# Two row tiles through each column group: a new opening for the projection stage of a hybrid decoder step

## The reference

```python
xn = rmsnorm(x, g_attn)                       # 1088 rows of 1024
z = xn @ w_in                                 # 1024 x 1952
cq  = rmsnorm(z[..., :256], g_q_a);   q = cq @ w_q_b          # 256 x 768, its last 32 columns a head rotated
ckv = rmsnorm(z[..., 256:384], g_kv_a); k, v = ckv @ w_uk, ckv @ w_uv   # 128 x 512 each
kr = rope(z[..., 384:416])                    # one key part for all heads
dq, dk, dv = rope(z[..., 416:928]), rope(z[..., 928:1440]), z[..., 1440:]
```

## Time and profile before

| | |
|---|---|
| Time, median of 3 runs (lowest to highest) | 1854.7 us (1853.81 to 1857.46) |
| The profiled execution | 1853.93 us, of which the span is 1852.4 |
| PE busy | 1733.5 us, 94% of the span |
| DVE, ACT, POOL busy | 861.0, 660.3, 573.8 us |
| First matmul of attention starts at | 281.07 us |

### The profile page before, as it was taken

How to read it: one execution, slowest core, us unless ns; L and a number is a source line. 1 busy time by engine, 2 the same in 40 slices (tenths; PEclk the granted TensorE clock), 3 DMA queues, 4 the chain that set the end, 5 groups by cost and what they waited for, 6 DMA issues and landing times.

```text
span 1852.4 us, 28046 instructions
## 1 busy us (share of the span) xinstructions
PE 1733.5 (94%) x9955; PEld 1509.9 (82%) x9955; DVE 861.0 (46%) x1802; ACT 660.3 (36%) x1329; POOL 573.8 (31%) x533
## 2 busy tenths in 40 slices
PE   3999988899996999999699999999999999999997
PEld 2788877888885888888578988898898888888985
DVE  5443325676773777667444233323333333233235
ACT  5222215576664766666322311112121121121213
POOL 0000003565662578678200312122122122131221
PEclk9999997999996999999899999999999999999998
DMA  7223213332315765654531495695875865956822
GB/s 254 83 95 103 84 55 105 94 95 55 100 34 143 197 195 157 164 149 132 178 110 29 114 171 106 132 145 130 149 118 131 172 103 113 167 122 135 135 55 101
DMA packets 156123, 227.41 MB, mean 123 GB/s; under 512 B 31127, under 2 KB 129048, under 8 KB 149592
## 3 DMA queue, kind: packets, MB, share of 16 engines
q1 hardware_dynamic: 153150, 159.39, 29.3%
q0 software_dynamic: 2880, 66.85, 22.1%
HBM read 201.12 MB, written 91.93 MB: 158 GB/s over the span
## 4 chain that ended last, share of the span: by engine, by line
PE 48%; DMA 2%; DVE 1%; ACT 1%; POOL 0%; issue 0%; ACTq 0%; SPq 0%; DVEq 0%; POOLq 0%
PE wide L2259 21%; PE turn L2281 14%; PE rest L2260 7%; PE wide L1942 5%; DMA acc<-in_w_gate 1%; DMA out_y_prompt<-f_gc 1%; PE wide L2357 0%; PE turn L1954 0%; DVE f_gc L2237 0%; ACT f_gc L2174 0%; DMA o_work<-scratch_s_o 0%; PE rest L2266 0%; DVE o_tl L1890 0%; POOL f_gl L2336 0%; ACT f_rows L2181 0%
## 5 line engine op out<-in xcount | busy, mean ns | idle before, releaser
L2194 DVE TENSOR_TENSOR acc<-turn,acc 128x512 f32<-128x512 f32 x198 | 136.6, 691 | 206.7 <-PE turn L2281 206.7
L2281 PE MATMUL turn<-f_dh,f_ah 128*128 128x512 f32 x396 | 158.3, 400 | 4.4 <-DVE f_al L2225 4.0
L2062 POOL TENSOR_TENSOR f_gl<-f_graw,f_gh 128x1024 fp32r<-128x1024 f32 x21 | 50.6, 2407 | 358.6 <-ACT f_gh L2112 358.6
L2281 PE MATMUL turn<-f_dl,f_ah 128*128 128x512 f32 x396 | 157.9, 399 | 0.0
L2281 PE MATMUL turn<-f_dh,f_al 128*128 128x512 f32 x396 | 157.9, 399 | 0.0
L2208 DVE SCALAR_TENSOR_TENSOR f_gc<-wide,f_coef,f_gc 128x832 f32<-128x832 f32 x44 | 47.7, 1085 | 209.3 <-ACT f_lasts L2132 206.4
L523 PE MATMUL zp<-win_h,xT_h 128*128 128x512 f32 (+1 forms) x288 | 112.6, 391 | 0.0
L1573 POOL TENSOR_TENSOR w_vl<-w_v,w_vh 96x2048 fp32r<-96x2048 f32 (+3 forms) x32 | 111.5, 3495 | 2.0
L523 PE MATMUL zp<-win_l,xT_h 128*128 128x512 f32 (+1 forms) x288 | 111.5, 387 | 0.0
L523 PE MATMUL zp<-win_h,xT_l 128*128 128x512 f32 (+1 forms) x288 | 111.4, 387 | 0.0
L2076 POOL TENSOR_TENSOR f_dl<-f_draw,f_dh 128x2048 fp32r<-128x2048 f32 x11 | 50.7, 4612 | 152.8 <-ACT f_dh L2152 152.8
(11 more groups left out here) (354 smaller groups left out, 4775.6 us busy)
## 6 DMA issues: line engine op xcount, KB each, us to landing
out_s_win_k<-in_state_win_k POOLq DMA_DIRECT2D x10, 3264.0 KB, 43.0
out_s_win_v<-in_state_win_v POOLq DMA_DIRECT2D x10, 3264.0 KB, 45.3
w_k<-in_state_win_k SPq DMA_DIRECT2D x16, 768.0 KB, 8.3
w_v<-in_state_win_v SPq DMA_DIRECT2D x16, 768.0 KB, 6.1
f_uraw<-in_w_up SPq DMA_DIRECT2D x22, 512.0 KB, 4.3
f_draw<-in_w_down SPq DMA_DIRECT2D x11, 1024.0 KB, 33.7
f_graw<-in_w_gate SPq DMA_DIRECT2D x21, 512.0 KB, 7.3
m_c<-in_cache_kv_latent SPq DMA_DIRECT2D x128, 64.0 KB, 1.8
```

Source lines behind the costliest of these rows:

```text
L2062: nc.gpsimd.tensor_tensor(w_lo[n][:], w_raw[n][:], w_hi[n][:].bitcast(F32), ALU.subtract)\
L2194: nc.vector.tensor_tensor(a, dp[h][:], a, ALU.add).then_inc(S["d_add"], 1)
L2281: last = nc.tensor.matmul(dp[h][:], a[:, c, t * P:(t + 1) * P], w[:, c, h * 512:(h + 1) * 512], start=(c == 0 and j == 0), stop=(c == 1 an ...
```

## The change

Only `project` changes. Five things:

- Tiles 0 and 1 go through each column group one after the other. Each has two banks: tile 0 uses `zp[0]` and `zp[1]` (groups 0 and 2, and 1 and 3), tile 1 uses `zp[2]` and `zp[3]`. From tile 2 on each group has its own bank as before.
- In tile 0 PE waits slice by slice, not group by group.
- On ACT and DVE the splits of the slices are woven between the other work of tiles 0 and 1. `w_uk` and `w_uv` now come before groups 2 and 3.
- The slots are four buffers of their own: `stage`, `dvm` (values), `turn` (rotation), `dqk`. `qm` and `km` are no slots any more. So queries and latents are built while slices still come; what is built in `dvm`, `turn` and `dqk` comes after slice 19. The sum of squares of tile 1 uses `dqk` as scratch, so slice 3 waits for it.
- SP issues what is needed first: `x` of tile 0, `g_x`, `ident`, `x` of tile 1, slices. The latents' gains and the rotary tables come later.

The loop `walk` then runs tiles 2 to 5, and 6 to 8 are written out.

```diff
+        banks = lambda t: [zp[i] for i in ((0, 1, 0, 1) if t.first else (2, 3, 2, 3) if t.second else range(4))]
-        need = {0: 4, 1: 8, "q": 10, 2: 14, 3: 18, "kv": 20}
+        need = {0: 0, 1: 4, "q": 10, "kv": 12, 2: 12, 3: 16}
+            return (stage, dvm, turn, dqk)[n % SLOTS][:, 0:a * b].rearrange("p (a b) -> p a b", a=a)
...
+                elif n == SLOTS - 1:
+                    sp.wait_ge(S["x_ms"], 2)
...
             def lead():   # scalar
-                square(Step.of(0))
-                weights(0, 4)
-                prep(Step.of(0))
-                weights(4, 8)
-                square(Step.of(1))
-                prep(Step.of(1))
-                weights(8, len(loads))
+                square(t0); square(t1); weights(0, 1); prep(t0); weights(1, 4); prep(t1); weights(4, 6)
+                sums(t0); weights(6, 8); latent_hi(t0); weights(8, 10); sums(t1); weights(10, 12)
+                key_turned(t0); query(t0); weights(12, 16); square(Step.of(2)); weights(16, 20)
+                act.wait_ge(S["w_lo"], len(loads))
+                key_value(t0); latent_hi(t1); key_turned(t1); query(t1); sliding_value(t0)
+                prep(Step.of(2)); square(Step.of(3)); key_value(t1); sliding_value(t1)
...
             def lead():   # vector, new
+                normalize(t0); weights(0, 1); normalize(t1); prep(t0); weights(1, 4); prep(t1); weights(4, 7)
+                latent(t0); weights(7, 8); latent_lo(t0); key_turned(t0); weights(8, 12)
+                latent(t1); query(t0); key_turned(t1); weights(12, 16); normalize(Step.of(2)); weights(16, 20)
+                dve.wait_ge(S["w_lo"], len(loads))
+                latent_lo(t1); sliding(t0, 0); sliding(t0, 1); query(t1); sliding(t1, 0)
+                prep(Step.of(2)); sliding(t1, 1); normalize(Step.of(3))
...
             def lead():   # tensor, new
+                prep(t0); prep(t1); rows_ready(t0); group(t0, 0); rows_ready(t1); group(t1, 0)
+                latent(t0); group(t0, 1); query(t0); group(t1, 1); key_value(t0); group(t0, 2)
+                latent(t1); group(t1, 2); query(t1); group(t0, 3); prep(Step.of(2)); key_value(t1); group(t1, 3)
```

More of the change, by code:

```diff
@@ L165, in project @@
 def project(nc, sem, io):
+    SLOTS = 4
     ctx = ExitStack()
@@ L214, in project @@
                               win_l[:, k0:k0 + 2, c0:c0 + n], (2, n)))
[L215 to L218, removed]
+        group_loads(0)
+        group_loads(1)
+        for k in range(2):
+            loads.append((io["w_q_b"].rearrange("(k p) n -> p k n", p=P)[:, k:k + 1], wqb_h[:, k:k + 1],
+                          wqb_l[:, k:k + 1], (1, HEADS * QK)))
         for i, n in enumerate(("w_uk", "w_uv")):
@@ L368, in prep, with sums @@
                     nc.scalar.copy(xT_h[t.odd][:, 4 * i:4 * i + 4, :], xp[i][:]).then_inc(S["xT_hi"], 1)
-            def main(t):
+            def sums(t):
+                z = banks(t)[0]
                 act.wait_ge(S["z0_ps"], t.n + 1)
@@ L487, in main, with sliding @@
-                if not ends(t):
-                    normalize(t.after_next())
+            def sliding(t, i):
+                dve.wait_ge(S[f"z{i + 1}_ps"], t.n + 1)
+                if not t.first:
+                    dve.wait_ge(S[("o_dq", "o_dk")[i]], t.n * 16)
+                if i == 1:
+                    dve.wait_ge(S["dq_ok"], t.n + 1)
+                elif not t.first:
+                    dve.wait_ge(S["dk_ok"], t.n)
+                rotate(heads(banks(t)[i + 1][:]), heads(dqk[:, i * HW:(i + 1) * HW]), heads(rt[0]), heads(rt[1]),
+                       rot[t.odd][:, 0:3 * RD], RD, "d_a", t.n * 6 + (3 * i + 3), ("dq_ok", "dk_ok")[i])
@@ L526, in product, with rows_ready, latent @@
                     last.then_inc(S[done], 1)
+            FREE = ("kr_ok", "dq_ok", "dk_ok", "dv_ok")
             def group(t, g):
                 c0, n = GROUPS[g]
-                if t.first:
-                    pe.wait_ge(S["w_lo"], need[g])
-                else:
-                    for s in (("kr_ok",), ("dq_ok",), ("dk_ok",), ("dv_ok",))[g]:
-                        pe.wait_ge(S[s], t.n)
-                product(zp[g][:, 0:n], [(xT_h[t.odd][:, k, :], xT_l[t.odd][:, k, :], win_h[:, k, c0:c0 + n],
-                                         win_l[:, k, c0:c0 + n]) for k in range(KC)], f"z{g}_ps")
-            def main(t):
+                z = banks(t)[g]
+                if t.first or t.second:
+                    if g >= 2:
+                        pe.wait_ge(S[FREE[g - 2]], t.n + 1)
+                else:
+                    pe.wait_ge(S[FREE[g]], t.n)
+                for k in range(KC):
+                    if t.first and k % 2 == 0:
+                        pe.wait_ge(S["w_lo"], need[g] + k // 2 + 1)
+                    xh, xl, wh, wl = (xT_h[t.odd][:, k, :], xT_l[t.odd][:, k, :], win_h[:, k, c0:c0 + n],
+                                      win_l[:, k, c0:c0 + n])
+                    for i, (a, b) in enumerate(((xh, wh), (xh, wl), (xl, wh))):
+                        last = nc.tensor.matmul(z[:, 0:n], a, b, start=(k == 0 and i == 0),
+                                                stop=(k == KC - 1 and i == 2))
+                last.then_inc(S[f"z{g}_ps"], 1)
+            def rows_ready(t):
                 pe.wait_ge(S["xT_lo"], t.n * 2 + 2)
-                group(t, 0)
-                group(t, 1)
+            def latent(t):
                 pe.wait_ge(S["cn_ok"], t.n + 1)
@@ L548, in main, with query @@
                 last.then_inc(S["cT_ps"], 1)
-                group(t, 2)
+            def query(t):
                 pe.wait_ge(S["cT_lo"], t.n + 1)
@@ L562, in main, with lead @@
                                                   wkv_l[:, c0:c0 + 512])], done)
-            staged(pe, prep, main)
+            def main(t):
+                rows_ready(t)
+                group(t, 0)
+                group(t, 1)
+                latent(t)
+                group(t, 2)
+                query(t)
+                group(t, 3)
+                key_value(t)
+            def lead():
+                t0, t1 = Step.of(0), Step.of(1)
+                prep(t0)
+                prep(t1)
+                rows_ready(t0)
+                group(t0, 0)
+                rows_ready(t1)
+                group(t1, 0)
+                latent(t0)
+                group(t0, 1)
+                query(t0)
+                group(t1, 1)
+                key_value(t0)
+                group(t0, 2)
+                latent(t1)
+                group(t1, 2)
+                query(t1)
+                group(t0, 3)
+                prep(Step.of(2))
+                key_value(t1)
+                group(t1, 3)
+                pe.wait_ge(S["dk_ok"], 1)
+                pe.wait_ge(S["dv_ok"], 1)
+            walk(pe, prep, main, lead)
 class Ring:
```

292 lines of the change are left out of this document (208 added, 84 removed).

## The result

The changed kernel takes 1835.12 us (median of 4 runs, 1830.51 to 1837.34) against 1854.26 us; the ratio is 0.9896, 95% interval 0.9875 to 0.9918. On another chip it came to 1834.12 against 1851.54, ratio 0.9915 (0.9888 to 0.9943). The forecast was 1836.1.

A forecast was written before the change was run, and what follows sets the result against it. PE was taken to set the projection phase's end; first product 16.6, work 52.6, stall 3.0, small waits 0.3 and clock 0.8 gave 73.3 against 91.9, so 1836.1 us, range 1829 to 1843.

The forecast's parts named there:

- What bounds the kernel: PE sets the end of the projection phase; whatever time tile 2 starts earlier, everything behind it starts earlier.
- T: Start of PE's transposes of tile 3, at 91.90 us before the change and forecast at 73.3.
- S: Start of tile 0's first product on PE, forecast at 16.6 us, with 15.6 and 17.6 as bounds.
- the bound of 10.2: Time in us for the cast of slice 0 if its load moves up by four small loads' issue; 11.0 was taken.
- The pause: PE's stall before tile 1's latents, waiting for ACT's copy of values behind the last splits; 3.0 us.
- The clock: Time lost to PE's lowered clock after the stall before tile 1's latents: 0 or 1.6 us, taken as 0.8.
- The sign set for being wrong: Granted clock of 0.50 for more than 7 us between the first product and tile 3's transposes.
- The sum: Start of tile 3's transposes: 16.6 + 52.6 + 3.0 + 0.3 + 0.8 = 73.3 us, a gain of 18.6.
- Slices too slow: Rival: DVE's eight late slices take 1.68 us each, stall 6.1, gain 13.7, about 1841 us; chance 0.18.
- no pause: Rival in the opening: first product at 15.6, stall 1, no clock loss, gain 22.4, 1832.3 us; chance 0.07.
- The clock stays low: Rival: PE's broken stream in the lead runs at 1.2 GHz, 26 us slower, 1881 us; chance 0.03.
- The entry of attention: Rival: the 17.0 us low clock there changes; at best 1829 us, at worst 1.3 us more; chance 0.08.

The follow-up runs named there:

- the value buffer: Against the changed kernel, tile 0's values get a buffer of their own and ACT copies them before slices 16 to 19; 1825.96 us, second run 1826.25.
- the second profile: The changed kernel itself, nothing altered, run and profiled again on another chip; 1834.12 us, ratio 0.9915 to the kernel before.
- the kernel with one tile at a time: Against the changed kernel, the pairing is undone: PE takes tile 0 through all its groups, then tile 1; 1839.85 us, ratio 0.9950 to before.
- the warm kernel: Against the early-start kernel, PE does ten unused transposes of the identity before the first product; 1824.33 us, second run 1824.58.
- the early-start kernel: Against the value-buffer kernel, tile 0's group 0 starts before tile 1 is normalized, with tile 1's transposes inside it; 1824.39 us, second run 1824.21.

## Why the prediction was right

*What bounds the kernel.* Right. PE's 52.64 us of work for two tiles behind the start gives T where there is neither a pause nor a low clock behind the start: 15.1 + 52.6 is 67.7 against 67.21 measured with the value buffer. And a shift of T is a shift of the end, as far as the medians tell.

*S.* Forecast 16.6, measured 15.25, below the lower bound of 15.6. The chain from the cast of slice 0 was sized right (5.48 for 5.6). The load was not: the cast came at 9.77 for 11.0. I had gone by bytes in the queue; with the old order of loads it came at 12.21, so the small and repeated loads (tables, gains) cost 2.4 us though they are 336 KB. SP issues slice 0's load at 2.89 for 4.79, so 1.9 of the 2.4 is the time to issue four loads, which I had worked out and used only as the bound of 10.2. The rows of tile 1 count too: they arrive at 8.72 for 10.95, and ACT squares them for 1.06 us just ahead of the cast.

*The pause.* Place, releaser and kind right; forecast 3.0, measured 4.15 and 3.68. The earlier S moves both ends of the pause, so they are counted from S: PE came after 30.95 us for the 31.5 forecast, and ACT's copy ended after 34.96 for 34.4. The four last splits took 1.28 us each, the pace I had taken and not the 1.68; but DVE waited 1.20 us ahead of them, and 0.84 in the second profile, for slices that were not there yet. The load of slice 16 was issued at 37.39, as soon as its slot was free, and took 5.5 us. The forecast had put this at nothing ("if slices are there when wanted"). Less this wait, an estimate, the pauses would have been 2.95 and 2.84 us.

*The clock.* Taken at 0.8 with 1.6 as the bound. Half of 4.51 us, 2.25, is what the first profile shows, and 1.65 the second (mean 0.64 over 4.60). Both are over the bound. It was half of the 3.20 us in which PE worked at 0.50 before; but there the clock had been low for some 3.6 us of the idle time already (mean 0.79 over 8.60), so less of the low time fell on work. The sign set for being wrong was more than 7 us at 0.50; with some 2 us inside the pause the low stretch of the first profile was about 6.8 us long.

*The sum.* 73.3 forecast, 73.99 and 72.81 measured. The misses cancel in part: S -1.35 and -1.5, the pause +1.15 and +0.7, the clock +1.45 and +0.85, PE's work and small waits -0.5 each time. That the sum is off by no more than 0.7 is in part luck. The gain on T was 18.6 forecast and is 17.9 and 19.1. Attention's first matmul came at 263.72 and 262.79, for about 262.5.

*The rivals.* Slices too slow, and no pause, did not come, apart from the late load of slice 16. "The clock stays low" did not come either: the granted clock is 1.00 over 30.95 us without a gap. The Trainium skill's warning of banks taken in turn ("TensorE: Matmul & The Clock Gate", "A second HAM failure mode: psum-queue depth-cycling") does not show where the groups follow without idle time, as in this trace; in the kernel with one tile at a time, whose gaps are waits for ACT and DVE and not for banks, the broken stream stays at 0.51 for 10.2 us. The entry of attention stayed much as it was: the 17.0 us from 270.8 on are at 0.51 for the 0.50 of before.

## What to carry to other kernels

Where weights are loaded and prepared in the opening, give the multiplying engine a second piece of data for each weight that arrives, and put the preparation of weights between the other engines' dependent steps: with the same early start, the woven preparation alone brought 11 to 13 us, the second piece of data alone nothing, both together 17 to 19. Then look who waits for the last slice only because its result lies in a staging slot; moving one small buffer out gave 8 us more. And price a pause twice, once as idle time and once by the clock behind it, here 1.6 to 2.25 us.

## What the hardware showed

In one of two profiles transposes alone brought PE to full clock. The level is read here from the distance between the starts of like matmuls, 0.19 us at full clock and 0.35 at half; the granted clock reads 1.00 from 8.6 us on in all these profiles, also where the starts are 0.35 apart. In the warm kernel PE had done nothing but 18 transposes when the first product began. In its second profile the products start 0.19 us apart from the second on; in its first they start 0.35 apart or more up to 14.15, and full clock came just behind that. In the early-start kernel, which lacks only the ten extra ones, they start 0.35 apart for over 4 us; in the value-buffer kernel, where eight transposes stand right ahead of the first product, for two. PE's timeline in the warm kernel's second run:

```profile
8.69 1.94 PE L675 MATMUL xp<-ident_sb,xn 128*128 128x128 f32 x8 [8.69 <-DVE xn L552]
10.43 2.34 PE L751 MATMUL zp<-ident_sb 128*128 128x128 f32 x10
12.93 0.46 PE L706 MATMUL zp<-win_h,xT_h 128*128 128x416 f32 x1 [0.17 <-DVE xT_l L558]
13.23 0.35 PE L706 MATMUL zp<-win_l,xT_h 128*128 128x416 f32 x1
13.42 0.35 PE L706 MATMUL zp<-win_h,xT_l 128*128 128x416 f32 x1
```

In the early-start kernel's second run:

```profile
12.83 0.72 PE L706 MATMUL zp<-win_h,xT_h 128*128 128x416 f32 x1 [2.30 <-DVE xT_l L558]
13.35 0.55 PE L706 MATMUL zp<-win_l,xT_h 128*128 128x416 f32 x1
...
16.82 0.55 PE L706 MATMUL zp<-win_h,xT_l 128*128 128x416 f32 x1
17.16 1.37 PE L675 MATMUL xp<-ident_sb,xn 128*128 128x128 f32 x8
```

And in the value-buffer kernel's second run:

```profile
15.84 0.55 PE L703 MATMUL zp<-win_l,xT_h 128*128 128x416 f32 x1
16.19 0.55 PE L703 MATMUL zp<-win_h,xT_l 128*128 128x416 f32 x1
...
17.47 0.35 PE L703 MATMUL zp<-win_h,xT_h 128*128 128x416 f32 x1
17.66 0.35 PE L703 MATMUL zp<-win_l,xT_h 128*128 128x416 f32 x1
```

The Trainium skill says the opposite ("TensorE: Matmul & The Clock Gate", "Part 4: PE-mode transpose": full clock does not engage for transposes). The measurement decides, for these 32-bit transposes.

A pause at the same place does not bring the clock down each time: at 3.14 us it stayed at 1.00, at 3.68, 3.99 and 4.15 us it fell, for 3.4, about 6.8 and about 6.8 us. Whether length or chance decides, these four do not tell. The fall need not come inside the pause. In the first profile of the changed kernel it came some two us before PE resumed; in the second the whole pause reads 1.00, and PE's matmuls went from 0.23 to 0.43 us apart only at 51.1, 1.3 us after it had resumed (stretches of that profile):

```profile
46.10:49.80 3.70, 0.04 (x1) 0.01 (x1) 2.43 (x2) 2.12 (x3) 0.00 (x0) 1.00 0.00 0
49.80:54.40 4.60, 4.58 (x15) 3.74 (x16) 3.30 (x8) 0.89 (x2) 0.00 (x0) 0.64 0.37 142
```
